# A two-block transformer kernel on one core: x's squares, one weight group and the rotary angles change places at its start

## The reference

```
m_lat = (silu(c) @ w_mod + b_mod).reshape(B, 1, 6, D)
m_ctx = (silu(c_ctx) @ w_mod + b_mod).reshape(6, D)
h_lat = rms_norm(x, norm_mix) * (1 + m_lat[:, :, 1]) + m_lat[:, :, 0]
h_ctx = rms_norm(ctx, norm_mix) * (1 + m_ctx[1]) + m_ctx[0]
... = split(h_lat @ w_in)      # and the same of h_ctx
x_mix = x + m_lat[:, :, 2] * merge_branches(...) @ w_out
...
ang = positions[..., None] * inv_freq      # cos and sin, used in the two later blocks
```

## Time and profile before

| | |
|---|---|
| median of 3 executions | 3019.33 us (3018.06 to 3019.4) |
| profiled execution | 3020.79 us, span 3019.0 us |
| mean granted TensorE clock | 0.988 |
| busy: TensorE, VectorE, ScalarE, GpSimd | 96%, 51%, 39%, 11% of the span |
| first projection matmul | 70.73 us |
| output projection | about 804 to 851.6 us |

### The profile page before, as it was taken

The page is one execution under the profiler, slowest core; times in us unless marked ns, Lnnn a source line. Parts: engine busy times, 40 slices in busy tenths (PEclk is TensorE's granted clock), DMA queues, the critical chain, the costliest instruction groups (busy, mean ns, idle before and its releaser), DMA issues. The chain is left out here.

```text
span 3019.0 us, 36895 instructions
## 1 busy us (share of the span) xinstructions
PE 2887.4 (96%) x14944; PEld 2297.5 (76%) x14944; DVE 1552.2 (51%) x2115; ACT 1180.9 (39%) x1735; POOL 325.1 (11%) x274
## 2 busy tenths in 40 slices
PE   7999999999999999899999999999999999999998
PEld 2889767678878888686687878888686778778886
DVE  2467256666544443447853454443458663554443
ACT  3642434442233332434643343332525643333332
POOL 0020024310001110001200021100102101111100
PEclk8999999999999999999999999999999999999999
DMA  6200210035422222221032112222120132122221
GB/s 245 70 29 1 81 53 29 29 136 177 148 79 94 94 96 98 79 70 43 29 110 87 70 70 98 97 107 98 56 84 15 49 119 70 58 96 98 97 98 56
DMA packets 45411, 250.07 MB, mean 83 GB/s; under 512 B 4816, under 2 KB 6992, under 8 KB 18896
## 3 DMA queue, kind: packets, MB, share of 16 engines
q1 hardware_dynamic: 45264, 248.01, 23.3%
HBM read 245.89 MB, written 2.10 MB: 82 GB/s over the span
## 5 line engine op out<-in xcount | busy, mean ns | idle before, releaser
L262 DVE TENSOR_TENSOR ring_lo<-ring,ring_hi 128x2048 fp32r<-128x2048 f32 x199 | 457.8, 2301 | 708.3 <-ACT ring_hi L255 708.1
L313 PE MATMUL bank<-h_hi,ring_hi 128*128 128x512 f32 x1360 | 545.8, 401 | 18.6 <-PEq L371 8.7
L255 ACT ACTIVATE ring_hi<-ring 128x2048 fp32r<-128x2048 f32 x199 | 379.9, 1909 | 415.9 <-PE bank L313 351.1
L313 PE MATMUL bank<-h_hi,ring_lo 128*128 128x512 f32 x1360 | 533.8, 392 | 0.0
L1600 PE MATMUL bank<-h_hi,ring_hi 128*128 128x512 f32 x960 | 374.6, 390 | 5.7 <-DVE ring_lo L262 5.7
L1603 PE MATMUL bank<-h_lo,ring_hi 128*128 128x512 f32 x960 | 374.0, 390 | 0.0
L1604 PE MATMUL bank<-h_hi,ring_lo 128*128 128x512 f32 x960 | 373.9, 389 | 0.0
L313 PEld LDWEIGHTS bank<-h_hi,ring_hi 128*128 128x128 f32 x1360 | 257.3, 189 | 78.0 <-DVE ring_lo L262 10.4
L313 PEld LDWEIGHTS bank<-h_hi,ring_lo 128*128 128x128 f32 x1360 | 257.0, 189 | 55.0
L313 PE MATMUL bank<-h_lo,ring_hi 128*128 128x512 f32 x624 | 245.9, 394 | 0.0
L1600 PEld LDWEIGHTS bank<-h_hi,ring_hi 128*128 128x128 f32 x960 | 180.3, 188 | 45.4 <-DVE ring_lo L262 8.2
(11 more groups left out here) (435 smaller groups left out, 4923.0 us busy)
## 6 DMA issues: line engine op xcount, KB each, us to landing
ring<-in_stream SPq DMA_DIRECT2D x201, 1024.0 KB, 4.8
mod_w<-in_stream SPq DMA_DIRECT2D x64, 256.0 KB, 3.3
xT<-in_xT SPq DMA_DIRECT2D x2, 2048.0 KB, 15.2
ring<-in_stream SPq DMA_DIRECT2D x7, 512.0 KB, 4.1
ring<-in_stream SPq DMA_DIRECT2D x10, 256.0 KB, 4.0
const<-in_const SPq DMA_DIRECT2D x1, 2306.5 KB, 15.6
memT<-in_memT SPq DMA_DIRECT2D x2, 1024.0 KB, 5.7
out<-xT SPq DMA_DIRECT2D x8, 256.0 KB, 2.0
```

The costliest lines, as they stand in the source:

```text
L255: nc.scalar.activation(self.slab_hi(slab + j), self.slab(slab + j), ACT.Copy).then_inc(slab_rounded, 1)
L262: nc.vector.tensor_tensor(lower, self.slab(slab + j), self.slab_hi(slab + j).bitcast(F32), ALU.subtract)\
L313: ins = nc.tensor.matmul(out, lhsT, rhs, start=start and w is w_hi and x is x_hi, stop=stop and w is w_lo)
```

## The change

1. Of the four groups of the modulation that the first stage needs, TensorE does three (`MOD_BY_PE`), from six slabs. The fourth group's two slabs are loaded into `h_spare`, and VectorE multiplies and adds them for both columns into `acc`; TensorE reduces `acc` with ones.
2. x is loaded in two halves behind slab 5. ScalarE squares it in the modulation stage, VectorE adds the eight squares, one fp32 matmul with ones sums over partitions, and the root is taken there. projC is told so (`given=True`) and does no squares or sums of x; its warming passes stay.
3. projC's first slab is rounded and split at the end of the modulation stage, and its second slab is rounded there. The second slab is split in projC, before the fifth product of h (`halfway_at`). With `by_two`, `four_tiles` does tiles 0 and 1 for the first five feature tiles, waits for the second slab, and does tiles 2 and 3.
4. Only 512 KB of the constants and their last five columns are loaded in the first stage; the levels' masks (1 MB) are loaded at the start of projC ahead of the context, and the columns called reset are no longer loaded.
5. The positions are loaded in the output projection's stage; VectorE computes the angles there in two pieces, before the outputs of tiles 2 and 4, and ScalarE the sines before tile 6.

The diff, cut to its core:

```diff
+MOD_BY_PE = 3
+FIRST_SLABS = MOD_FIRST * KT // SLAB
+BY_DVE_SLABS = FIRST_SLABS - MOD_BY_PE * 4 * KT // SLAB
...
             def four_tiles(pe):
-                ws.first_two(pe, first_slab())
+                if by_two:
+                    pe.wait_ge(slab_split, ws.count(first_slab()) - WHOLE_SLABS)
+                else:
+                    ws.first_two(pe, first_slab())
...
-                for k in range(TOGETHER):
-                    for n in range(4):
-                        first = part_of(n, k)
+                for few in ((0, 1), (2, 3)) if by_two else (range(4),):
+                    if by_two and few[0]:
+                        ws.first_two(pe, first_slab())
+                    for k in range(TOGETHER):
+                        for n in few:
+                            first = part_of(n, k)
...
+                        if n == 0 and k == self.halfway_at and self.halfway_vector:
+                            self.halfway_vector(dve)
...
+        def load_levels(sp):
+            at = slice(CONST["levels"], CONST["reset"])
+            sp.dma_start(const[:, at], const_in[:, at]).then_inc(levels_loaded.sem, 16)
...
             def sync(sp):
                 sp.dma_start(par1[:, :], par1_in).then_inc(params_in.sem, 16)
+                for n in range(BY_DVE_SLABS):
+                    ws.feed(sp, n + 1)
+                    sp.dma_start(h_spare[:, 4 * n:4 * n + 4, :]..., stream[WHOLE_SLABS + n])\
+                        .then_inc(acc_loaded[n].sem, 16)
                 ws.feed(sp, RING)
-                sp.dma_start(const[:, :], const_in).then_inc(inputs_loaded.sem, 16)
-                sp.dma_start(xT[:, :, :], xT_in).then_inc(inputs_loaded.sem, 16)
-                sp.dma_start(pos_i[:, :], pos_in.to_broadcast([P, T])).then_inc(inputs_loaded.sem, 16)
+                sp.dma_start(const[:, 0:C_FIRST], const_in[:, 0:C_FIRST]).then_inc(inputs_loaded.sem, 16)
+                sp.dma_start(const[:, CONST["freq"]:CONST_W], const_in[:, CONST["freq"]:CONST_W]).then_inc(inputs_loaded.sem, 16)
+                ws.feed(sp, WHOLE_SLABS)
+                for n in range(2):
+                    sp.dma_start(xT[:, 4 * n:4 * n + 4, :], xT_in[:, 4 * n:4 * n + 4, :]).then_inc(x_loaded[n].sem, 16)

             def scalar(act):
...
+                logs_with_exps(act)
...
+                for g in range(MOD_BY_PE - 1):
+                    row(g)
+                for k in range(KT):
+                    if k % 4 == 0:
+                        act.wait_ge(x_loaded[k // 4].sem, x_loaded[k // 4].at(16))
+                    nc.scalar.activation(hT[:, k, :], xT[:, k, :], ACT.Square).then_inc(x_squared.sem, 1)
+                row(MOD_BY_PE - 1)
+                act.wait_ge(inputs_loaded.sem, inputs_loaded.at(32))
+                act.wait_ge(x_summed.sem, x_summed.at(1))
+                root_of_mean(act, x_scales[:, 0, :], bank[:, 5, :])
+                ws.round_to(act, WHOLE_SLABS + 1, RING_SLABS)

             def tensor(pe):
...
+                def reduce():
+                    pe.wait_ge(acc_ready.sem, acc_ready.at(1))
+                    for e in range(4):
+                        for s in range(2):
+                            at = 2 * (4 * MOD_BY_PE + e) + s
+                            nc.tensor.matmul(bank[:, 0, at:at + 1], acc[:, s, e * P:(e + 1) * P], con("ones", 1), start=True, stop=True)
...
+                pe.wait_ge(inputs_loaded.sem, inputs_loaded.at(32))
+                for g in range(MOD_BY_PE - 1):
+                    turn(g)
+                reduce()
+                turn(MOD_BY_PE - 1).then_inc(mod_done.sem, 1)
+                pe.wait_ge(x_added.sem, x_added.at(1))
+                nc.tensor.matmul(bank[:, 5, :], con("ones"), hT[:, 0, :], start=True, stop=True).then_inc(x_summed.sem, 1)

             def vector(dve):
...
+                for k in range(KT):
+                    if k % 4 == 0:
+                        dve.wait_ge(acc_loaded[k // 4].sem, acc_loaded[k // 4].at(16))
+                    if k:
+                        dve.drain()
+                    for s in range(2):
+                        w, c = h_spare[:, k, :], sc[:, k, s:s + 1]
+                        if k == 0:
+                            nc.vector.tensor_scalar(acc[:, s, :], w, c, None, ALU.mult)
+                        else:
+                            last = nc.vector.scalar_tensor_tensor(acc[:, s, :], w, c, acc[:, s, :], ALU.mult, ALU.add)
+                last.then_inc(acc_ready.sem, 1)
+                for k in range(1, KT):
+                    dve.wait_ge(x_squared.sem, x_squared.at(k + 1))
+                    if k > 1:
+                        dve.drain()
+                    last = nc.vector.tensor_tensor(hT[:, 0, :], hT[:, 0, :], hT[:, k, :], ALU.add)
+                last.then_inc(x_added.sem, 1)
                 dve.wait_ge(mod_done.sem, mod_done.at(1))
...
+                ws.halve_to(dve, WHOLE_SLABS, RING_SLABS)
...
             def load_context(sp):
+                load_levels(sp)
                 sp.dma_start(ctxT[:, :, :], ctxT_in).then_inc(ctx_in.sem, 16)
...
-                squares, scales, load_context, loaded=(1, ctx_in), splits=[(h, 0), (hc, KT)])
+                squares, x_scales, load_context, loaded=(1, ctx_in), splits=[(h, 0), (hc, KT)], given=True)
...
+            def sines(act):
+                act.wait_ge(angles_ready.sem, angles_ready.at(2))
...
-                   banks=7, operands=[merged_parts], also={("dve", 0): mod_end}, pe_also={0: lambda pe: mod_reduce(pe, MOD_GROUPS - 1)})
+                   banks=7, operands=[merged_parts], sync=load_positions,
+                   also={("dve", 0): mod_end, ("dve", 2): lambda dve: angles(dve, 0), ("dve", 4): lambda dve: angles(dve, 1),
+                         ("act", 6): sines}, pe_also={0: lambda pe: mod_reduce(pe, MOD_GROUPS - 1)})
```

More of the change, by code:

```diff
@@ L427, in wait, with linear @@
                 eng.wait_ge(self.by[engine].sem, self.by[engine].at(ordinal))
-        def linear(name, tiles, banks=8, sync=None, operands=(), last_split=None, norm=None, also=None, pool_also=None, pe_also=None, outs=None, busy=0):
+        def linear(name, tiles, banks=8, sync=None, operands=(), last_split=None, norm=None, also=None, pool_also=None, pe_also=None, outs=None, busy=0, by_two=False):
             n_act = sum(t[0] == "act" for t in tiles)
@@ L2411, in turn @@
                     return last
+                def reduce():
[4 more added lines that the diff above has]
+                            nc.tensor.matmul(bank[:, 0, at:at + 1], acc[:, s, e * P:(e + 1) * P], con("ones", 1), start=True, stop=True)
                 pe.wait_ge(c_ready.sem, c_ready.at(1))
[L2413 to L2415 removed]
+                for g in range(MOD_BY_PE):
@@ L2874, in load_mod @@
                     slab, part = divmod(m, 4)
-                    sp.dma_start(mod_w[:, m % MOD_BUFFERS, :], stream[WHOLE_SLABS + slab][:, part * 512:(part + 1) * 512])\
+                    sp.dma_start(mod_w[:, m % MOD_BUFFERS, :], stream[FIRST_SLABS + slab][:, part * 512:(part + 1) * 512])\
                         .then_inc(mod_loaded[m % MOD_BUFFERS].sem, 16)
@@ L2913, in residual, with load_positions, angles @@
                                                                       xT[:, n, :], ALU.mult, ALU.add)
+            pos_i = same_place("pos_i", "part", [P, T], I32)
+            ang = mod_w
+            pos_loaded = Signal("pos_loaded", 16)
+            angles_ready = Signal("angles_ready", 2)
+            def load_positions(sp):
+                sp.dma_start(pos_i[:, :], pos_in.to_broadcast([P, T])).then_inc(pos_loaded.sem, 16)
+            def angles(dve, n):
+                two_pi = 2 * np.pi
+                parts, left = [], two_pi
+                for bits in (7, 15):
+                    part = np.floor(left * 2.0 ** bits) / 2.0 ** bits
+                    parts.append(float(np.float32(part)))
+                    left -= parts[-1]
+                parts.append(float(np.float32(left)))
+                magic = 1.5 * 2.0 ** 23
+                a, r = ang[:, n, :], ang[:, 2, :]
+                if n == 0:
+                    dve.wait_ge(pos_loaded.sem, pos_loaded.at(16))
+                    nc.vector.tensor_copy(ang[:, 3, :], pos_i[:, :])
+                    dve.drain()
+                nc.vector.tensor_scalar(a, ang[:, 3, :], con("freq", 1, n), None, ALU.mult)
+                dve.drain()
+                nc.vector.tensor_scalar(r, a, 1.0 / two_pi, magic, ALU.mult, ALU.add)
+                dve.drain()
+                nc.vector.tensor_scalar(r, r, magic, None, ALU.subtract)
+                dve.drain()
+                for part in parts:
+                    nc.vector.scalar_tensor_tensor(a, r, -part, a, ALU.mult, ALU.add)
+                    dve.drain()
+                nc.vector.tensor_scalar(a, a, -3.1415925, 3.1415925, ALU.max, ALU.min).then_inc(angles_ready.sem, 1)
@@ L2914, in build_program @@
+            def sines(act):
+                act.wait_ge(angles_ready.sem, angles_ready.at(2))
```

(6 more changed lines are left out.)

91 lines of the change are left out of this document (27 added, 64 removed).

## The result

The changed kernel takes 2997.76 us (median of 4 runs, 2996.19 to 3001.42), the kernel before 3019.36 (4 runs, 3018.06 to 3020.19). The ratio is 0.9931, with a 95% interval of 0.9913 to 0.9948: faster by 0.7%, 21.6 us. The forecast was 2996, with 2993 to 3001 as its range.

The account below looks back on a forecast made before the run. From the first projection matmul on, TensorE was taken as the bound, so its earlier start counts: 70.73 - 47.35 = 23.4 us, angles 0. 3020.79 - 23.4 = 2997.4, less 1.46: 2995.9, said 2996, range 2993 to 3001.

Parts of the forecast that it names:

- Loads: Head: slab 0 to end of x takes 23.0 us plus 0.7; x's halves in at 27.6 and 30.0 us.
- the load of short rows: Head: the constants' last five columns, 128 rows of 20 bytes, cost 0.7 us, with bounds 0 and 1.3.
- the rival of a late x: Head: later loads share the engines and delay x by up to 4.8 us; gain 18.6 us, 3001 us; chance 0.08.
- TensorE: Modulation: 0.7 us wait for slab 2, slabs 2 to 5 done at 29.7 us, reduction 2.0, free at 33.3 to 35.0.
- the rival of a falling clock: Head: the clock falls in the load waits, five slabs take 6.85 us each; gain 6 us, 3013 us; chance 0.08.
- VectorE's adds, sum, root, split: End of modulation: seven adds end at 34.2 us, sum of x 35.5, root 36.95, slab 6's split 41.25.
- the forecast's high side: Total up to 2999 us: reduction and sum at half clock 1.0 (sum 1.7), 0.6, warm-up 0.3, hand-overs some 1 us.
- The angles: Output projection: VectorE's 9.2 us and ScalarE's 4.9 us are hidden, cost 0; at most 14.1 us if uncovered.
- The warm-up: Start of the first projection: 32 warming passes, 3.73 us at full clock or 6.1 from half; 5.8 us taken.
- Cover check: First projection: third lower half ready at 49.25 us, TensorE wants it at 50.1 and doesn't wait; four tiles take 21.9 us.
- if the third lower half is waited for: First projection: a sign of being wrong, TensorE waiting for the third lower half of h, which was forecast ready at 49.25 us.
- later stages give the time back: Behind the head: a sign of being wrong, the first projection matmul is early but later stages lose the gain; no size given.

Follow-up runs that it names:

- after_again: The changed kernel run once more, unaltered, in a second series on another chip: 3000.76 us (5 runs), ratio 0.9933 to the kernel before.
- by_one: The changed kernel with the four tiles done together for each feature tile, as before, instead of two by two: 2998.48 us, ratio 0.9929.
- pool_late: The changed kernel with GpSimd's add over the levels' masks held back until the first row of keys: 2999.61 us, one execution.
- split_early: The changed kernel with the second slab's split back ahead of the wait for the root, in all norms but the first projection's: 2998.12 us, one execution.
- round_first: The changed kernel with ScalarE rounding slab 6 before it waits for the sum of x, not after the root: 2997.85 us, one execution.
- sums_later: The changed kernel with x's squares, sums and root back in the projection's stage, and the four tiles in the old order: 3004.32 us, ratio 0.9948.
- angles_only: The kernel before with only the positions, angles and sines moved to the output projection: 3007.47 us against 3019.65, ratio 0.9959.
- gap_warm: The changed kernel with 48 more warming passes behind the sum of x, in the modulation stage: 3001.24 us, one execution.
- group_by_pe: The changed kernel with all four modulation groups on TensorE, eight slabs, and none on VectorE: 3001.87 us, ratio 0.9938.
- best1: The changed kernel with late mask add, early split elsewhere, 48 gap warming passes, 24 instead of 32 behind, slab 7 split before eighth product: 2995.16 us, ratio 0.9921.
- after: The changed kernel itself, in its first series and profile: 2997.76 us (median of 4 runs), ratio 0.9931; profiled execution 2998.34 us.

## Why the prediction was right, and where it wasn't

The time and its main mechanism were right: a gain of 23.4 us at the head was forecast, 23.3 came. The changed kernel's second series, after_again, has its median at 3000.76 us, 19.4 below the kernel before; that is still in the range of 2993 to 3001, but at its edge, and two of its five executions lie above it. By its steps:

- **Loads.** x's halves at 27.6 and 30.0 forecast; their squares begin at 28.07 and 30.53. Slab 0 was 0.9 us later in this execution, so the transfers between took 0.4 us less than the sum had, and of the 0.7 us for the load of short rows some 0.3 are left. (It landed at 20.8, 1.3 us behind the 512 KB ahead of it, but not all of that delayed x.) Slabs 6 and 7, issued later, didn't hold x up, so the rival of a late x didn't come true.
- **TensorE.** Last weight pass 29.7 forecast, 30.8 measured: 0.9 is slab 0's start, 0.4 one more pass of 0.85 us than the five assumed, 0.2 the pace of the four slabs behind it, and the wait for slab 2 was 0.25 us and not 0.7. Reduction 2.0, measured 1.95. The clock did not fall in that wait, so the rival of a falling clock didn't come true; a load wait of 0.7 us didn't occur.
- **VectorE's adds, sum, root, split.** 34.2, 35.5, 36.95 and 41.25 forecast; 34.54, 35.73, 37.21 and 41.33 measured. The sum took 1.13 us here, at full clock; in after_again, by_one, pool_late, split_early and round_first it took 2.07 or 2.08, at half, which is beyond the forecast's high side of 1.7. In those, slab 0 came earlier than at 7.21, and the next stage starts at the same 41.5 to 41.8 us (39.38 in round_first). sums_later shows what this block is worth, 6 us at the first matmul.
- **The angles.** Cost 0 forecast. First to last output of the output projection takes 38.08 us in both kernels, the sines end 3.9 us ahead of the last output, and angles_only keeps all of its gain.
- **The warm-up.** 5.8 us forecast, 6.02 measured. It is no fixed price: with the clock already full it took 3.81 in gap_warm.

The experiments split the 23.3 us only in part: 10.5 for the angles (from the kernel before), 6.05 for squares and sums and 2.5 for the group on VectorE (both from the changed kernel). If these add up, some 4.2 us are left to edits that no run has alone, fewer constants in the head and slab 6 split a stage early among them.

Two things failed.

*The step "Cover check"*: "the third lower half is ready at 41.55 + 7.7 = 49.25; TensorE, with two tiles per step (1.37 us), wants it at 50.1. It doesn't wait." It was ready at 51.1 and TensorE waited 0.73 us; the four tiles took 22.98 us, not 21.9. VectorE's chain was right instruction by instruction, but GpSimd was left out. Its add over the masks waits for the levels, whose load the change moves to the next stage's start, so that it lands in the middle of VectorE's products, and the one holds the other up (0.75 becomes 2.62 us, and GpSimd's own 2.69). pool_late takes the add away and the loss with it. The prediction named only the transfers behind that load, the context's, and not the engine that waits for it. Among its own signs of being wrong was "if the third lower half is waited for", and that one came true. The Trainium skill (SBUF — State Buffer, "SBUF: two separate sides") says that a VectorE instruction with two inputs from SBUF, the on-chip memory, and a GpSimd instruction that reads SBUF share a pair of ports by an exclusive lock: whoever starts first has it for the whole instruction, and the other is blocked and doesn't share. The traces agree. GpSimd's add, begun at 47.89, would by that rule have to wait for VectorE's product to end at 48.60 and then run its 2.08 us to 50.68; it ended at 50.58, and VectorE's next at 51.13, 0.55 us behind it. The same order stands in the six other traces in which the two meet (after_again, by_one, group_by_pe, split_early, gap_warm, round_first): the blocked VectorE instruction takes 2.57 to 2.61 us and ends 0.54 to 0.56 us behind the add, wherever the add began.

*A missed edit.* The prediction, and the description of the change ahead of it, take the new line with `halfway_at` as the first projection's business alone. It serves all norms, and where `halfway_at` is 0 the call still moved behind the wait for the root: 2.2 us in the first block's feed-forward, undone by split_early. Of the prediction's signs of being wrong, "later stages give the time back" so came true for these 2.2 us.

Neither shows in the total as it should, for the second warm-up was 2.3 us shorter than in the profile before, which the prediction didn't have. 23.3 − 1.1 + 2.3 − 2.2 gives 22.3, and the span shrank by 22.5 (the smaller steps of the ledger cancel). So part of the agreement is luck. With both omissions in it, the forecast would have been 2995.9 + 1.1 + 2.2 = 2999.2, which also lies among the runs of the changed kernel (2996.19 to 3003.35 in the two series). What stays open is why the second warm-up was longer before. Its 36 passes took 6.59 us in the one profile of the kernel before, 5.88 in pool_late and best1, and 4.26 in the ten others, after_again and angles_only among them. No kernel was profiled both ways, so it isn't shown whether this is chance or hangs on the moment at which the stage begins.

## What to carry to other kernels

When a load moves, list every engine that waits for it, the idle ones too: GpSimd's one instruction had nothing to do with the stage, and it held VectorE up for 1.9 us at the one place where TensorE was waiting for it. When a shared helper gets a new parameter, read what the default value now does in every other caller. And an engine freed early is only worth what its next operand allows: ahead of such a gain, find the next wait. In gap_warm a start 1.8 us earlier ended in a wait of 2.92 us, a fall of the clock and four tiles that ended 2.0 us later. And work put into an idle stretch must fit it at the clock that it will get: 48 passes of 0.117 us at full clock took 7.15 us there, not 5.6.

## What the runs showed of the hardware

- An elementwise instruction of VectorE with operands of 128x512 took 0.75 us alone and 2.57 to 2.62 us behind a GpSimd add of 128x896, in seven traces. The add took 2.08 to 2.14 us alone. Where it began while a VectorE instruction still had 0.14 to 0.72 us to run, it took 2.12 to 2.69, that is 0.04 to 0.61 more than 2.08, and by and large the more the more was left.
- A wait of about 3 us in a stage with a full clock can end with the clock at half or not. Behind 2.92 us (gap_warm, third lower half) it was at 0.50 for about 3.5 us; in the 2.98 us ahead of sums_later's first matmul it fell to 0.50 and stayed there up to 59 us. But the 2.98 us ahead of the feed-forward's first matmul (after at 843.11, after_again at 845.87) left it at 1.00 up to 854 us. Waits of 0.73 us (after), 1.01 (after_again) and 1.50 (round_first) for the third lower half left it at 1.00 too.
- The second warm-up, 36 passes of the same code in kernels that differ elsewhere, took 4.26, 5.88 or 6.59 us; of one kernel only one of these was seen. But a dip of the clock worth 2.7 us does stand in one profile of the changed kernel and not in the other. So two profiles of one kernel can differ by as much as an edit of this size.
